# GpSimd walks the side chains' gathers three steps behind its slots, and TensorE waits for the selected rows sample by sample

## The chip, the cores and the metric

The kernel is one program on one core of a Trainium2 chip. The metric is device time in microseconds, the median of the runs; lower is better. The profiler's record of one execution gives the rows below.

## The reference

One layer of a decoder is computed for 512 prompt tokens and for 8 sample tokens, each sample with a paged cache of 4096 past tokens. Cut to what matters here:

```python
# samples: three attentions, each after a choice that depends on scores
score = einsum(relu(q_idx . k_idx_all) * w_idx);  top_i = top_k(score, 256)
kv = gather_paged(cache_a_kv, page_table, kv_a, top_i)         # branch A: 256 rows per sample
o_cmp, sel, sel_ok = nsa_compressed(q_b, qpos, kv_c, ...)      # compressed blocks, top 16 blocks
o_slc = nsa_selected(q_b, qpos, sel, ..., gather_paged(cache_slc_kv, ...))   # 16 blocks of 64 tokens
o_win = nsa_window(...); o_m = memory_attend(q_m, cache_mem_kv)
# prompt: expert retrieval, 512 tokens x 8 heads x 16 experts
a = gelu(einsum('nhkd,nd->nhk', u_tab[e], xb));  out = einsum('nhk,nhkd->nd', g * a, v_tab[e])
```

## The kernel before

**The slot stream.** The prompt's experts are mixed in 512 slots: 4 tiles of 128 tokens, 128 experts per token. For slot `s` GpSimd issues one indirect DMA (L3256) that brings, for each of the 128 tokens, one row of 8 KB (the expert's row of `u_tab` and of `v_tab` side by side), so 1.05 MB per slot. It lands in one of `NBUF` = 7 buffers, which lie in space that other tiles left (`ex_pairs`, `heads_t`, `branch_rows_t`, `cmp_k_t`, `cmp_v`); the rows call the gathers by these names. VectorE multiplies and sums the u half with the token (L3288, "the dot"), ScalarE makes the coefficient one step later, and `LAG` = 3 steps later the v half is added: by VectorE (L3283) or, for some slots, by TensorE with a diagonal matrix (L3350). A buffer is free when slot `s - 7` is dotted and added. So GpSimd can issue the gather of slot `s` as soon as the add of slot `s - 7` is done, which VectorE or TensorE does at its step `s - 4`: GpSimd runs up to four steps ahead.

**The side chains.** The rest of the layer is spread between the slots. `Beside` holds a chain of stages, each with a first and a last step; a stage is a generator per engine, which yields the fraction of its steps at which its next piece is due. At step `s` each engine first calls `advance(..., s)`, which emits all pieces due by then, and then does its own work of slot `s`. A stage begins with a wait for all engines that took part in the stages before it (`ended`). There are two chains, `beside` and `aside`; each engine runs its instructions strictly in order. From slot 317 on the chain `beside` is the samples' attention, and this is where GpSimd has pieces of its own:

- `INDEX` (28 steps): loads of index keys, `is_ch` (L2221), four at the stage's start, then 12 more, each into a ring of 4; TensorE transposes each of them. Chunk `u` is due on GpSimd at `(u - 1) / 17` of the stage, on TensorE at `(u + 0.5) / 17`.
- `SELECT` (36 steps): three iotas (L2362) for the 256 keys to be chosen, and from the end of it 16 small gathers `sk_t` (L2182, one step each), which VectorE reads in `place_keys` (L2470), 14 steps on.
- `da_rows`: 32 gathers of the chosen keys, values and biases (`da_kv`, `da_bias`), spread over `DSA_ROWS` = 30 steps; then 16 gathers `sl_bias`.
- `sl_gather`: 16 gathers of 0.52 MB each (`sl_kv`, and the last four into `cmp_k_t` and `cmp_v`), two per step over 8 steps, for the attention over the selected blocks, `sl_at` (`SEL_AT` = 40 steps). At its end GpSimd waits until all 16 have landed, and the next stages wait for GpSimd.
- on `aside`: two loads of the window's keys and values, 2.1 MB each (L2623), from slot 348 on, and later the ring of memory keys and values (L2662), 0.5 MB each.

Of `attend_samples` the change uses an argument that other calls use already:

```python
def turn(u):
    b, j, m = units[u]
    for sem, value in (waits(b) if waits else ()):
        pe.wait_ge(sem, value)
```

Of the kernel before, what the change touches and what calls it, by code (L numbers as in the profile page):

```python
# [19 lines left out]
SEQ, DB, PAST, PAGE = 512, 8, 4096, 128  # L20
# [5 lines left out]
DH, HQ, KV, GRP = 64, 8, 2, 4  # L26
# [5 lines left out]
BLK, NBLK, NSEL = 64, PAST // 64, 16  # L32
# [47 lines left out]
RETRIEVE_HALF, RETRIEVE_NEXT, MERGE, TURN, LINEAR, NORM, RETRIEVE_LAST = 22, 40, 64, 4, 16, 9, 64  # L80
WEIGHTS, COMPRESS, INDEX, SELECT = 6, 72, 28, 36
WINDOW_FROM, WIN_AT, MEMORY, CMP_AT, DSA_AT, SEL_AT = 348, 16, 70, 14, 18, 40
DSA_ROWS = 30
ROW_MOVES = 200
NBUF, NDIAG = 7, 4
LAG, SETTLE, RELOAD = 3, 4, 60
# [141 lines left out]
class Kernel:  # L228
# [1876 lines left out]
    def sample_dsa(self, ctx, sl_rows, sl_bias, sl_bias_rows, qz, nsa):  # L2105
            nc, i, s = self.nc, self.i, self.s
# [3 lines left out]
            kv = self.sb("da_kv", [P, 2, DB, KV * 2 * DH], F32, ctx)  # L2110
# [10 lines left out]
            with tmp:  # L2121
                prob = self.sb("cm_prob", [DB * HQ, NCH_S + DB], F32, tmp)
                sk = ExitStack()
                with sk:
                    chosen = self.select_keys(sk)
                    self.attend_samples("cm_at", NCMP_S, HQ, qz, keys=lambda b: self.kc_t[:, b, :NCMP_S],
                                        values=lambda b, j: self.vc[:min(P, NCMP_S - P * j), b, j].rearrange("p g d -> p (g d)"), acc=nsa, turned=False,
                                        bias=self.bias_cmp, prob=prob, gate=self.gate_bh[:, 0:1], add=True, behind=[windowed], steps=CMP_AT, scoring=0.3)
                    self.place_keys(chosen, phys, past_ix, is_new)
                rows_at = self.beside.next_step  # L2130
                landed = self.gather("da_rows", [(kv[:, n // DB, n % DB, :], i["cache_a_kv"].rearrange("n p w -> (n p) w"), phys[:, n:n + 1]) for n in range(2 * DB)]
                            + [(bias[:, n // DB, n % DB, :], s["bias_pos"], past_ix[:, n:n + 1]) for n in range(2 * DB)], apart=True, steps=DSA_ROWS, behind=windowed)
                self.pick_blocks(prob, sl_rows, sl_bias_rows)
                self.beside.next_step = rows_at + DSA_ROWS
            sl_bias_in = self.gather("sl_bias_rows", [(sl_bias[:, BLK * n:BLK * n + BLK], s["bias_head"].rearrange("h (b t) -> (h b) t", t=BLK), sl_bias_rows[:, n:n + 1])
                                                      for n in range(NSEL)], apart=True, steps=18)

# [4 lines left out]
            with nc.psum_tensor("da_h_ps", [P, 512], F32) as h_ps, self.block() as block:  # L2142
# [18 lines left out]
                def _(pe):  # L2161
# [4 lines left out]
                                values=lambda b, j: kv[:, j, b, KV * DH:], acc=out_a,  # L2166
                                waits=lambda b: landed if b == 0 else (), bias_t=lambda j: bias_a[:, DB * j:DB * j + DB].rearrange("p b h -> p (b h)"), own=0, own_bias=0, own_mask=own_hit,
                                out0=0, steps=DSA_AT, scoring=0.4)
            return sl_bias_in

    def gather(self, tag, jobs, depth=4, apart=False, steps=None, behind=None):

        sems = [self.gather_sem(f"{tag}_in{n}") for n in range(min(depth, len(jobs)))]
        landed = [(sem, 16 * len(range(n, len(jobs), depth))) for n, sem in enumerate(sems)]
        with self.block(steps or len(jobs) * 3 // 7, apart) as block:
            @block.gpsimd
            def _(pool):
                if behind:
                    pool.wait_ge(*behind)
                for n, (dst, table, rows) in enumerate(jobs):  # L2180
                    yield n / len(jobs)
                    pool.indirect_dma_start(out=dst, out_offset=None, in_=table,  # L2182
                                            in_offset=bass.IndirectOffsetOnAxis(ap=rows, axis=0)).then_inc(sems[n % depth], 16)
                if not apart:
                    for sem, count in landed:
                        pool.wait_ge(sem, count)
        return landed
# [298 lines left out]
    def sample_slc(self, rows, bias, bias_in, qz, nsa):  # L2486
        i = self.i
        ctx = ExitStack()
        NG = DB * KV
        with ctx:  # L2490
            kv_new = self.sb("sl_kv", [P, NG - 2 * KV, OCT * 2 * DH], F32, ctx)
            old = [x.rearrange("p (g w) -> p g w", g=KV) for x in self.compressed_space()]
            rows_of = [kv_new[:, n:n + KV] for n in range(0, NG - 2 * KV, KV)] + old
            kv = [x.rearrange("p g (d c j) -> p c j (g d)", c=2, j=OCT) for x in rows_of]
            self.gather("sl_gather", [(rows_of[n // KV][:, n % KV], i["cache_slc_kv"].rearrange("n q w -> (n q) w"), rows[:, n:n + 1]) for n in range(NG)],
                        steps=8, behind=(self.aside.ended, self.aside.before))
            dropped = self.sem("sl_dropped")
            with self.block() as block:
                @block.vector
                def _(dve):  # L2500
                    for sem, count in bias_in:
                        dve.wait_ge(sem, count)

                    dve.memset(bias[:, BLK * (NSEL - 1):], NEG).then_inc(dropped, 1)
            self.attend_samples("sl_at", NSEL * BLK, HQ, qz, keys=lambda b, j: kv[b][:, 0, j], values=lambda b, j: kv[b][:, 1, j], acc=nsa,
                                bias=bias.rearrange("p (q i) -> p i q", i=OCT), own=1, own_bias=1, own_mask=self.own_mask, gate=self.gate_bh[:, 1:2],
                                add=True, out0=4, steps=SEL_AT, scoring=0.65)

# [706 lines left out]
    def mix_prompt(self, idx, gate, dots, coef, pair, x, y, diag, y_ps, chosen, beside, aside, merged):  # L3215
# [12 lines left out]
        def at(n):  # L3228

            return n // SLOTS, n % SLOTS  # L3230
# [7 lines left out]
        with nc.Block() as block:  # L3238
            @block.gpsimd
            def _(pool):  # L3240
                for s in range(end):
                    beside.advance("gpsimd", pool, s)
                    aside.advance("gpsimd", pool, s)
                    if s < NS:
                        t, m = at(s)
                        if m == 0 or s == SLOTS // 2:
                            pool.wait_ge(chosen, t + 1 + (1 if s else 0))
                        if s == ROW_MOVES:
                            pool.wait_ge(beside.ended, merged)
                        if s >= NBUF:  # L3250
                            pool.wait_ge(dot_done, s - NBUF + 1)
                            if by_dve[s - NBUF]:
                                pool.wait_ge(acc_done, dve_upto[s - NBUF])
                            else:
                                pool.wait_ge(mix_done, pe_upto[s - NBUF])
                        pool.indirect_dma_start(out=pair(s), out_offset=None, in_=i["uv_tab"],  # L3256
                                                in_offset=bass.IndirectOffsetOnAxis(ap=idx[:, t, m:m + 1], axis=0)).then_inc(pair_in[s % NBUF], 16)
                beside.advance("gpsimd", pool, 10 ** 9)
                aside.advance("gpsimd", pool, 10 ** 9)
# [313 lines left out]
```

## Time and profile before

| | us |
|---|---|
| runs | 2791.97 median (2789.25, 2791.97, 2803.37) |
| the profiled execution | 2781.56, its span 2779.9 |
| VectorE busy | 1761.6 |
| TensorE busy (matmul) | 1812.3 |
| GpSimd busy | 864.9 |
| ScalarE busy | 670.4 |
| gathers by GpSimd, share of the 16 DMA engines' span | 52.0% |

Busy times are of the whole span. The slots run from 805 to 2632 us; ahead of them lie the prompt's projections and attention, behind them the samples' own experts. What is read below are therefore stretches: which engine or queue is full there, and what ends the idle time of the others.

### The profile page before, as it was taken

The page shows a single profiled execution, that of the slowest core. Times are in us where ns is not written, and L with a number is a line of the kernel's source. Part 1 is how long each engine was busy: PE and PEld are TensorE (multiplying, and loading weights), DVE is VectorE, ACT ScalarE, POOL GpSimd, SP SyncE. Part 2 cuts the span into 40 slices and gives each one's busy share as a digit, 9 for nine tenths or more (in the row PEclk, how much of TensorE's full clock was granted, in tenths as well). Part 3 has the DMA queues.
Part 4 walks back from the last instruction along what each step waited for, and adds up shares of the span by engine and source line. Part 5 has one row for each costly group of instructions (what it writes and reads, how often), then busy time and mean ns, then how long its engine had stood idle before and what let it go on. Part 6 is the DMA issues. An engine that isn't in the chain of part 4 may idle for free. (4 is left out here: it accounts for less than half of the span.)

```text
span 2779.9 us, 25050 instructions
## 1 busy us (share of the span) xinstructions
PE 1812.3 (65%) x6605; PEld 1000.1 (36%) x6605; DVE 1761.6 (63%) x3916; ACT 670.4 (24%) x2035; POOL 864.9 (31%) x829
## 2 busy tenths in 40 slices
PE   7999799699836738844467515665877533418374
PEld 3466476444412213312222114444743213304311
DVE  3343465711168967685789965666779688859813
ACT  2011266410113323321233211222222111214100
POOL 1000042200024723342353432221531477654301
PEclk9999799899969969977799957878568755555586
DMA  4122320043248989997998898996986799899863
GB/s 150 25 88 76 96 92 2 1 166 130 104 167 349 421 348 358 355 392 306 377 379 326 356 367 311 350 355 246 404 343 247 295 351 374 324 363 398 330 227 122
DMA packets 200920, 727.69 MB, mean 262 GB/s; under 512 B 39785, under 2 KB 83330, under 8 KB 133898
## 3 DMA queue, kind: packets, MB, share of 16 engines
q0 software_dynamic: 84384, 577.16, 52.0%
q1 hardware_dynamic: 115226, 144.70, 15.3%
q10 hardware_dynamic: 1168, 4.23, 0.4%
q8 instruction: 54, 0.88, 0.1%
q14 instruction: 88, 0.72, 0.1%
HBM read 717.42 MB, written 12.66 MB: 263 GB/s over the span
## 5 line engine op out<-in xcount | busy, mean ns | idle before, releaser
L3256 POOL DMA_INDIRECT ex_pairs<-in_uv_tab,e_idx x147 | 196.0, 1333 | 552.9 <-POOLq L3153 246.7
L3316 ACT ACTIVATE ex_coef<-ex_dots 128x1 f32<-128x1 f32 x512 | 103.6, 202 | 1046.8 <-DVE ex_dots L3288 953.9
L3256 POOL DMA_INDIRECT branch_rows_t<-in_uv_tab,e_idx x163 | 192.2, 1179 | 256.8 <-DVE heads_t L3283 160.4
L3256 POOL DMA_INDIRECT heads_t<-in_uv_tab,e_idx x146 | 186.0, 1274 | 268.4 <-DVE heads_t L3283 146.8
L1337 PE MATMUL cs_pp<-cs_ch,xn_t 128*128 128x256 f32 x512 | 146.3, 456 | 175.9 <-DMA cs_ch<-in_cache_cmp_kv 175.9
L3288 DVE CUSTOM_DVE_ANT_0 branch_rows_t<-branch_rows_t,heads_t 128x1024 f32<-128x1024 f32 x163 | 198.6, 1220 | 55.2 <-DMA branch_rows_t<-in_uv_tab,e_idx 50.3
L3288 DVE CUSTOM_DVE_ANT_0 ex_pairs<-ex_pairs,heads_t 128x1024 f32<-128x1024 f32 x147 | 179.5, 1222 | 60.9 <-DMA ex_pairs<-in_uv_tab,e_idx 58.9
L820 PE MATMUL in_acc<-in_w,xn_t 128*128 128x512 f32 (+7 forms) x560 | 208.1, 527 | 5.8 <-POOLq L178 4.0
L3288 DVE CUSTOM_DVE_ANT_0 heads_t<-heads_t 128x1024 f32<-128x1024 f32 x146 | 178.1, 1221 | 37.8 <-DMA heads_t<-in_uv_tab,e_idx 34.9
L1337 PEld LDWEIGHTS cs_pp<-cs_ch,xn_t 128*128 128x128 f32 x512 | 118.5, 235 | 205.9 <-DMA cs_ch<-in_cache_cmp_kv 106.8
L3283 DVE SCALAR_TENSOR_TENSOR heads_t<-branch_rows_t,ex_coef,heads_t 128x1024 f32<-128x1024 f32 x118 | 151.2, 1281 | 30.6 <-issue 14.7
L3318 ACT ACTIVATE ex_coef<-ex_coef,e_gate 128x1 f32<-128x1 f32 x512 | 150.8, 295 | 16.6
L3350 PE MATMUL ex_y_ps<-ex_pairs,heads_t 128*128 128x512 f32 x188 | 98.9, 657 | 76.9 <-ACT heads_t L3323 71.8
L3283 DVE SCALAR_TENSOR_TENSOR heads_t<-ex_pairs,ex_coef,heads_t 128x1024 f32<-128x1024 f32 x100 | 127.9, 1279 | 28.5 <-issue 24.9
L3283 DVE SCALAR_TENSOR_TENSOR heads_t<-heads_t,ex_coef 128x1024 f32<-128x1024 f32 x100 | 128.0, 1280 | 25.5 <-issue 22.2
L820 PEld LDWEIGHTS in_acc<-in_w,xn_t 128*128 128x128 f32 (+1 forms) x560 | 95.1, 174 | 108.3 <-issue 88.4
L3350 PE MATMUL ex_y_ps<-heads_t 128*128 128x512 f32 x184 | 99.0, 667 | 47.8 <-ACT heads_t L3323 38.6
L3350 PE MATMUL ex_y_ps<-branch_rows_t,heads_t 128*128 128x512 f32 x180 | 96.2, 666 | 31.8 <-ACT heads_t L3323 30.9
L1638 PE MATMUL at_t_ps<-at_diag,at_exp 128*128 128x128 f32 (+3 forms) x608 | 87.6, 288 | 21.7 <-POOL at_diag L1726 20.9
L2925 PE MATMUL fq_mg_g_ps<-fq_mg_wg,xn_t 128*128 128x512 f32 x192 | 85.0, 596 | 0.0
L3350 PEld LDWEIGHTS ex_y_ps<-ex_pairs,heads_t 128*128 128x128 f32 x188 | 35.6, 205 | 135.5 <-ACT heads_t L3323 97.8
L1638 PEld LDWEIGHTS at_t_ps<-at_diag,at_exp 128*128 128x128 f32 (+3 forms) x608 | 71.9, 185 | 34.6 <-POOL at_diag L1726 22.0
(727 smaller groups left out, 3435.1 us busy)
## 6 DMA issues: line engine op xcount, KB each, us to landing
cs_ch<-in_cache_cmp_kv SPq DMA_DIRECT2D x256, 128.0 KB
fq_mg_wg<-in_w_gate SPq DMA_DIRECT2D x6, 2048.0 KB
in_w<-in_w_in SPq DMA_DIRECT2D x4, 2048.0 KB, 11.3
first_w<-in_w_gate SPq DMA_DIRECT2D x3, 2048.0 KB, 7.9
fp_wb<-in_w_branch SPq DMA_DIRECT2D x6, 1024.0 KB, 10.2
fp_wg<-in_w_gate SPq DMA_DIRECT2D x3, 2048.0 KB, 8.1
fq_mg_wb<-in_w_branch SPq DMA_DIRECT2D x6, 1024.0 KB
fs_mg_wb<-in_w_branch SPq DMA_DIRECT2D x6, 1024.0 KB, 9.8
```

What stands on the lines that cost most here:

```text
L820: last = pe.matmul(acc[:r, u % 2, :n], self.xT[:, k, P * t:P * t + r], w[:, j % 2, k, :n], start=(k == 0), stop=(k == KD - 1))
L1337: last = pe.matmul(pp[:, n % 2, 256 * c:256 * c + 256].rearrange("p (g k m) -> p g k m", g=KV, m=8), wts[:, c, r, :], ch[:, n % NBUF, :, c ...
L1638: last = pe.matmul(t_ps[:w, u % 2, k, :], ex[:, u % 6, P * k:P * k + w], diag[:, u % 4, :], start=True, stop=True)
L2925: last = pe.matmul(g_ps[:r, u % 2, :], xT[:, k, cols], wg[j % depth][:, k, :], start=(k == 0), stop=(k == KD - 1))
L3256: pool.indirect_dma_start(out=pair(s), out_offset=None, in_=i["uv_tab"], in_offset=bass.IndirectOffsetOnAxis(ap=idx[:, t, m:m + 1], axis=0 ...
L3283: dve.scalar_tensor_tensor(out=y(t), in0=v(n), scalar=coef[:, t, m:m + 1], in1=y(t), op0=ALU.mult, op1=ALU.add).then_inc(acc_done, 1)
L3288: dve.tensor_tensor_reduce(out=u(s), in0=u(s), in1=x(t), scale=1.0, scalar=0.0, op0=ALU.mult, op1=ALU.add, accum_out=dots[:, t, m:m + 1]). ...
L3316: act.activation(c, dots[:, t, m:m + 1], ACT.Gelu_apprx_tanh).then_inc(gelu_done, 1)
L3318: act.activation(c, c, ACT.Copy, scale=gate[:, t, m:m + 1]).then_inc(coef_done, 1)
L3350: last = pe.matmul(y_ps[:, q, :], diag[:, (pe_upto[n] - 1) % NDIAG], v(n)[:, 512 * q:512 * q + 512], start=n in first_pe, stop=n in last_pe)
```

## The change

Three edits, all in the order of work.

GpSimd's pieces of both chains are emitted with `s - BEHIND` in place of `s`, so three slot gathers later than before. `beside` gets `LANDING` = 5 more steps between the start of `da_rows` and what follows it. `sl_gather` no longer holds GpSimd until its rows have landed: it is a stage apart, each sample has a semaphore of its own, TensorE waits for it before the sample's transposes, and what follows it is put `SEL_ROWS` = 12 steps on (8 before).

```diff
-DSA_ROWS = 30
+DSA_ROWS, SEL_ROWS, LANDING, BEHIND = 30, 12, 5, 3
@@ sample_dsa
-                self.beside.next_step = rows_at + DSA_ROWS
+                self.beside.next_step = rows_at + DSA_ROWS + LANDING
@@ gather
-    def gather(self, tag, jobs, depth=4, apart=False, steps=None, behind=None):
+    def gather(self, tag, jobs, depth=4, apart=False, steps=None, behind=None, sems=None):
-        sems = [self.gather_sem(f"{tag}_in{n}") for n in range(min(depth, len(jobs)))]
+        sems = sems or [self.gather_sem(f"{tag}_in{n}") for n in range(min(depth, len(jobs)))]
-                                            in_offset=bass.IndirectOffsetOnAxis(ap=rows, axis=0)).then_inc(sems[n % depth], 16)
+                                            in_offset=bass.IndirectOffsetOnAxis(ap=rows, axis=0)).then_inc(sems[n * len(sems) // len(jobs) if len(sems) == DB else n % depth], 16)
@@ sample_slc
+            kv_in = [self.gather_sem(f"sl_rows_in{b}") for b in range(DB)]
-                        steps=8, behind=(self.aside.ended, self.aside.before))
+                        depth=DB, sems=kv_in, apart=True, steps=8, behind=(self.aside.ended, self.aside.before))
+            self.beside.next_step += SEL_ROWS
-            self.attend_samples("sl_at", NSEL * BLK, HQ, qz, keys=lambda b, j: kv[b][:, 0, j], values=lambda b, j: kv[b][:, 1, j], acc=nsa,
+            self.attend_samples("sl_at", NSEL * BLK, HQ, qz, keys=lambda b, j: kv[b][:, 0, j], values=lambda b, j: kv[b][:, 1, j], acc=nsa, waits=lambda b: [(kv_in[b], 16 * KV)],
@@ mix_prompt, gpsimd
-                    beside.advance("gpsimd", pool, s)
-                    aside.advance("gpsimd", pool, s)
+                    beside.advance("gpsimd", pool, s - BEHIND)
+                    aside.advance("gpsimd", pool, s - BEHIND)
```

The first place where GpSimd's own order changes is the start of `INDEX`. Its rows there before (slot gathers at L3256, a row with x2 is two of them):

```order
L3256 DMA ex_pairs<-in_uv_tab,e_idx 128x2048 x2
L2221 DMA is_ch<-in_cache_a_kidx,chunk_rows 128x1024 x4
L3256 DMA heads_t<-in_uv_tab,e_idx 128x2048 x2
L3256 DMA branch_rows_t<-in_uv_tab,e_idx 128x2048 x3
L2221 DMA is_ch<-in_cache_a_kidx,chunk_rows 128x1024
```

And now, where the slot gathers have line L3258:

```order
L3258 DMA ex_pairs<-in_uv_tab,e_idx 128x2048 x2
L3258 DMA heads_t<-in_uv_tab,e_idx 128x2048 x2
L3258 DMA branch_rows_t<-in_uv_tab,e_idx 128x2048
L2221 DMA is_ch<-in_cache_a_kidx,chunk_rows 128x1024 x4
L3258 DMA branch_rows_t<-in_uv_tab,e_idx 128x2048 x2
L3258 DMA ex_pairs<-in_uv_tab,e_idx 128x2048 x2
L3258 DMA heads_t<-in_uv_tab,e_idx 128x2048
L2221 DMA is_ch<-in_cache_a_kidx,chunk_rows 128x1024
```

Three slot gathers (317 to 319) moved ahead of the first index loads, and with them ahead of the wait for the stage before; every later index load stands three gathers further down too. TensorE's and VectorE's orders are unchanged here.

The second place is the end of the 16 small gathers `sk_t` and the start of `da_rows`. Before, with the memory ring's loads (`xn_t`) between:

```order
L2182 DMA sk_t<-tmp_cand,sk_cand_at 128x1
L3256 DMA branch_rows_t<-in_uv_tab,e_idx 128x2048
L2662 DMA xn_t<-in_cache_mem_kv 128x1024
L3256 DMA branch_rows_t<-in_uv_tab,e_idx 128x2048
L2182 DMA da_kv<-in_cache_a_kv,da_phys 128x256
L3256 DMA ex_pairs<-in_uv_tab,e_idx 128x2048
```

Now:

```order
L2182 DMA sk_t<-tmp_cand,sk_cand_at 128x1
L3258 DMA ex_pairs<-in_uv_tab,e_idx 128x2048
L2664 DMA xn_t<-in_cache_mem_kv 128x1024
L3258 DMA heads_t<-in_uv_tab,e_idx 128x2048
L2182 DMA da_kv<-in_cache_a_kv,da_phys 128x256
L3258 DMA heads_t<-in_uv_tab,e_idx 128x2048
```

The last `sk_t` stood ahead of the gather of slot 397 and stands ahead of that of slot 400 now, while VectorE's `place_keys`, which reads it, keeps its place at step 396.

The third place is the start of `sl_gather`. Before:

```order
L3256 DMA branch_rows_t<-in_uv_tab,e_idx 128x2048 x2
L2182 DMA sl_kv<-in_cache_slc_kv,sl_rows 128x1024
L3256 DMA ex_pairs<-in_uv_tab,e_idx 128x2048
L2182 DMA sl_kv<-in_cache_slc_kv,sl_rows 128x1024 x2
L3256 DMA ex_pairs<-in_uv_tab,e_idx 128x2048
```

Now:

```order
L3258 DMA branch_rows_t<-in_uv_tab,e_idx 128x2048
L3258 DMA ex_pairs<-in_uv_tab,e_idx 128x2048
L2182 DMA sl_kv<-in_cache_slc_kv,sl_rows 128x1024
L3258 DMA ex_pairs<-in_uv_tab,e_idx 128x2048
L2182 DMA sl_kv<-in_cache_slc_kv,sl_rows 128x1024 x2
```

The first `sl_kv` stood ahead of the gather of slot 448 and stands ahead of that of slot 456 now: five steps by `LANDING`, three by `BEHIND`. The attention that reads the rows starts at step 466 in place of 457, and ends at step 506 in place of 497; the slots end at 511.

## Rows read from the trace of the kernel before

**Rows 1.** Windows: slots before and in the samples' attention, and one full stretch.
```profile
core 0: us, PE busy (x) PEld busy (x) DVE busy (x) ACT busy (x) POOL busy (x), PEclk, DMA share, GB/s
805.00:1912.00 1107.00, 655.69 (x1734) 315.15 (x1735) 828.25 (x1704) 299.16 (x873) 417.14 (x317) 0.81 0.92 358
1912.00:2632.00 720.00, 389.74 (x1399) 260.25 (x1397) 559.75 (x1041) 163.16 (x562) 350.78 (x312) 0.60 0.86 337
1956.00:2035.00 79.00, 72.07 (x336) 69.88 (x336) 71.86 (x113) 18.67 (x62) 40.80 (x34) 0.50 1.02 419
```

**Rows 2.** Waits of GpSimd: line, what for, us in total, times, longest.
```profile
POOL is_ch L2221 <- DVEq L177: 31.7, 1, 31.7
...
POOL xn_t L2662 <- DVEq L177: 19.0, 1, 19.0
...
POOL sk_grid_i L2362 <- POOLq L178: 15.5, 1, 15.5
...
POOL sl_kv L2182 <- DVEq L177: 11.7, 1, 11.7
...
POOL sk_t L2182 <- DVEq L177: 7.3, 1, 7.3
```

**Rows 3.** Windows around these stalls, and one behind the third, columns as in Rows 1.
```profile
1920.00:1950.00 30.00, 14.93 (x60) 11.00 (x60) 16.03 (x40) 7.39 (x15) 5.14 (x6) 0.74 0.23 60
2042.00:2055.00 13.00, 8.29 (x16) 4.16 (x16) 8.80 (x38) 2.70 (x9) 2.44 (x5) 0.63 0.19 35
...
2140.00:2157.00 17.00, 7.56 (x35) 4.93 (x34) 15.44 (x48) 3.71 (x13) 0.51 (x1) 0.78 0.13 48
...
2167.00:2195.00 28.00, 14.48 (x25) 5.49 (x26) 19.62 (x55) 6.79 (x23) 4.99 (x5) 0.70 0.81 327
...
2420.00:2440.00 20.00, 0.40 (x4) 0.29 (x4) 10.34 (x19) 1.99 (x8) 6.45 (x8) 0.50 0.57 211
```

**Rows 4.** Timeline of VectorE, dots that waited: start, us, what, idle before.
```profile
1956.47 1.23 DVE L3288 CUSTOM_DVE_ANT_0 heads_t<-heads_t 128x1024 f32<-128x1024 f32 x1 [5.28 <-DMA heads_t<-in_uv_tab,e_idx]
...
2074.28 1.23 DVE L3288 CUSTOM_DVE_ANT_0 branch_rows_t<-branch_rows_t,heads_t 128x1024 f32<-128x1024 f32 x1 [9.73 <-DMA branch_rows_t<-in_uv_tab,e_idx]
...
2167.14 1.23 DVE L3288 CUSTOM_DVE_ANT_0 branch_rows_t<-branch_rows_t,heads_t 128x1024 f32<-128x1024 f32 x1 [9.47 <-DMA branch_rows_t<-in_uv_tab,e_idx]
...
2213.89 1.23 DVE L3288 CUSTOM_DVE_ANT_0 branch_rows_t<-branch_rows_t,heads_t 128x1024 f32<-128x1024 f32 x1 [4.28 <-DMA branch_rows_t<-in_uv_tab,e_idx]
...
2221.77 1.22 DVE L3288 CUSTOM_DVE_ANT_0 branch_rows_t<-branch_rows_t,heads_t 128x1024 f32<-128x1024 f32 x1 [2.58 <-DMA branch_rows_t<-in_uv_tab,e_idx]
...
2440.50 1.23 DVE L3288 CUSTOM_DVE_ANT_0 ex_pairs<-ex_pairs,heads_t 128x1024 f32<-128x1024 f32 x1 [7.16 <-DMA ex_pairs<-in_uv_tab,e_idx]
...
2484.49 1.22 DVE L3288 CUSTOM_DVE_ANT_0 ex_pairs<-ex_pairs,heads_t 128x1024 f32<-128x1024 f32 x1 [5.32 <-DMA ex_pairs<-in_uv_tab,e_idx]
```

**Rows 5.** Timeline of GpSimd: last `sk_t`; gathers of slots 398 and 456.
```profile
2254.56 0.95 POOL L2182 DMA_INDIRECT sk_t<-tmp_cand,sk_cand_at  x1 [0.30 <-issue]
...
2258.03 0.97 POOL L3256 DMA_INDIRECT branch_rows_t<-in_uv_tab,e_idx  x1 [0.30 <-issue]
...
2478.22 1.77 POOL L3256 DMA_INDIRECT ex_pairs<-in_uv_tab,e_idx  x1 [15.30 <-DVE ex_dots L3288]
```

**Rows 6.** Timeline of VectorE: `place_keys` reads `sk_t`.
```profile
2261.85 0.18 DVE L2470 TENSOR_SCALAR da_is_new<-sk_t 128x16 f32<-128x16 f32 x1 [1.47 <-DMA sk_t<-tmp_cand,sk_cand_at]
```

**Rows 7.** Timeline of GpSimd and VectorE: the gather of slot 338, and its dot.
```profile
2012.52 1.36 POOL L3256 DMA_INDIRECT heads_t<-in_uv_tab,e_idx  x1 [1.84 <-DVE heads_t L3283]
...
2024.81 1.22 DVE L3288 CUSTOM_DVE_ANT_0 heads_t<-heads_t 128x1024 f32<-128x1024 f32 x1
```

**Rows 8.** Timeline: an add, the last scores of `sl_at`, and the VectorE instruction behind.
```profile
2552.98 1.28 DVE L3283 SCALAR_TENSOR_TENSOR heads_t<-branch_rows_t,ex_coef,heads_t 128x1024 f32<-128x1024 f32 x1
...
2554.13 1.12 PE L1954 MATMUL sl_at_l_ps<-sl_at_kt,sample_qz 128*64 128x128 f32 x4
...
2555.46 2.03 DVE L2037 TENSOR_TENSOR sl_at_p<-sl_at_l_ps,sl_bias 64x512 f32<-64x512 f32 x2
```

## The prediction

> **What bounds the kernel now.** I read windows first, because the busy shares of the whole span mix stages. From 805 to 1912 us, before the samples' attention, the 16 DMA engines are 0.92 busy and VectorE 828 of 1107 us: transfers set the pace, GpSimd has no pieces of its own there, and the change moves nothing. From 1912 to 2632 the same two are at 0.86 and 560 of 720 us [rows 1]. No engine is full, DMA is not either, so the stretch holds gaps in which both stand still; TensorE, 390 of 720, is further off. In the full part of it, 1956 to 2035, DMA is at 1.02 with 419 GB/s and VectorE at 71.9 of 79 us [rows 1]: that is what the stretch looks like when nothing stalls.
>
> The waits come next. GpSimd waits once for each stage that it enters: 31.7 us for `is_ch` (`INDEX`), 19.0 for `xn_t` (the memory ring), 15.5 for `sk_grid_i` (`SELECT`), 11.7 for `sl_kv`, 7.3 for `sk_t` [rows 2]. Behind each stands the next slot gather. Windows around four such places show the DMA share at 0.23, 0.19, 0.13 and 0.57, the memory ring's being the emptiest [rows 3]; GpSimd's wait alone costs nothing, an empty DMA queue does. What it costs is read on VectorE, as the idle time that a dot spends on its rows: 5.28 us at 1956, 9.73 at 2074, 9.47 at 2167, 4.28 and 2.58 at 2214 and 2222, 7.16 at 2440, 5.32 at 2484 [rows 4]. The last of these follows GpSimd's hold for the 16 landings: its gather of slot 456 was issued after 15.30 us of idle time [rows 5].
>
> **The change, part by part.** With `BEHIND` = 3 GpSimd issues three more slot gathers before it comes to the same wait. The wait still ends when VectorE or TensorE end their stage, so GpSimd waits less, and DMA has 3 x 1.05 MB more to move meanwhile: at 419 GB/s that is 7.5 us of transfers. Where DMA is the pace behind the stall, 7.5 us bounds the gain; where it isn't, what bounds it is three slots' pace. From the dot of slot 317 (1956.47) to that of 338 (2024.81) a slot takes 68.3 / 21 = 3.25 us [rows 4, 7], so three are 9.8.
>
> The Trainium skill, page "DMA: Bandwidth & Descriptors", section "Where 436 GB/s comes from", puts the limit for transfers between HBM and SBUF at the HBM side, about 358 GB/s per core. By it three gathers would be 8.8 us, and the second term below 8.8 in place of 7.5, a sum 1.3 larger. The trace disagrees, with 419 GB/s over 79 us [rows 1], so I stay with 7.5.
>
> - `INDEX`: VectorE's idle time is 5.28 [rows 4], less than 7.5. Gain 5.3. Bounds: 2 (if the rest of the queue refills more slowly) and 7.5.
> - `SELECT`: idle 9.73, in front of it the window's two loads of 2.1 MB, which still stand ahead of slot 351's gather in the queue. So not the whole idle time goes: gain 7.5, the three gathers. Bounds 4 and 9.7.
> - Memory ring: idle 9.47 [rows 4], and behind it DMA is at 0.81 only [rows 3], so not the bound. Three slots' pace (9.8) covers it. Gain 9.5. Bounds 5 and 9.8.
> - First `sk_t`: 4.28 + 2.58 = 6.9 [rows 4], within 7.5. Bounds 3 and 7.5.
> - `sl_gather`: GpSimd comes to it later by three slots and by `LANDING`'s five steps, when what it waits for is over, and no longer holds for the landings. 7.16 + 5.32 = 12.5 [rows 4]. `LANDING` itself is free as long as slots are left to cover the attention that starts nine steps later: it ends at step 506 of 511. Bounds 7 (if TensorE and VectorE, which work in 9 steps fewer after it, give the landing part back) and 13.
>
> Sum of gains 41.7.
>
> Costs. The last `sk_t` was issued at 2254.56 and read by `place_keys` at 2261.85, after 1.47 us of waiting: 7.3 us from issue to use [rows 5, 6]. Now it stands behind the gather of slot 399, whose buffer is free after the add of step 395; the gather of 398 went out at 2258.03 [rows 5], and a step of dot and add is 1.23 + 1.28 = 2.5 us [rows 4, 8]: 2260.5, and with the same 7.3 us it is read at 2267.8, 6 late. VectorE stands still for it, with the dot behind. Meanwhile gathers go on, which gives back 1 by my estimate: cost 5. Bounds: 0 (the buffers fill, and VectorE catches up) and 9 (DMA's queue is longer by three gathers and the small one waits 1.5 + 7.5).
>
> TensorE now waits per sample in `sl_at`, in front of 64 groups of transposes. Scoring is a chain on TensorE at the granted clock 0.5, that is 1.2 GHz; its last matmul begins at 2554.13 and is followed at 2555.46 by the VectorE instruction that reads it [rows 8], so nothing is spare there. A wait that is long over costs TensorE a fraction of 0.1 us in a sequence with 64 of them: cost 1, between 0 and 4. The landed rows themselves have nine further steps, so the wait itself stays empty. In return GpSimd's hold goes, which is in the last gain.
>
> The other edits, which semaphore each `sl_kv` counts on, cost nothing: they are a number in an instruction that is there anyway.
>
> Sum: 41.7 - 5 - 1 = 35.7 us off the profiled execution of 2781.56: 2745.9. Its time stands 0.37% below the median of the runs shown, 2791.97; times that ratio, 2756.
>
> **The rivals.** *Waits go to VectorE.* The pieces that GpSimd issues late are read on time by others. If late landings at `INDEX` and at `sk_t` take back half of the first four gains (29.2 / 2 = 14.6), the gain is 21.1, the time 2771. For it: `place_keys` waits already now [rows 6]. Against it: the stages are 14 steps from issue to use elsewhere.
>
> *DMA is full anyway.* If the gathers that are issued ahead only stand longer in a queue that moves no more bytes, 2792. Against it: shares of 0.13 to 0.57 at the very places [rows 3]. For it: the share is 0.86 over the whole stretch [rows 1], and behind every stall the backlog is worked off at full rate.
>
> *More gain.* The buffers stay fuller behind each place, and small waits for gathers go too, of which 720 - 560 = 160 us of VectorE's idle time [rows 1] has many that I didn't count. If they give another 20, 2736.
>
> *The index ring starves (slower).* Chunk `u` is due on TensorE 1.5 / 17 of 28 steps, 2.5 steps, after GpSimd; with the four steps that GpSimd runs ahead this is 6.5, and three of them go. 3.5 slots x 3.25 = 11.4 us are left. A gather takes 12.3 us from issue to its dot, 2012.52 to 2024.81 [rows 7]: if a chunk takes as long in the queue, it is 0.9 late. From there VectorE (which copies each transpose) stops, its buffers aren't freed, and GpSimd issues the next chunk later still. With 12 refills it decides from (35.7 + 14) / 12 = 4.1 us each. At 5 us each the time is 2781.56 - 35.7 + 60, scaled 2816. Against it: the 12.3 hold time in which the rows had landed and the dot only waited its turn.
>
> The Trainium skill says on the same page, section "Two DMAs through the same engine are not ordered", that descriptors of one queue start in order, which would give a chunk the whole wait of the gathers ahead of it and speaks for this rival. The trace has a small `sk_t` landed 7.3 us after issue at the latest [rows 5, 6], with the gather of slot 397 and others around it, which is neither proof nor disproof.
>
> **How the numbers follow.** The forecast case has 60%, waits on VectorE 16%, DMA full anyway 8%, more gain 8%, the index ring 8%. 0.5% is 14 us and about what a measurement of this kernel tells from no change. The forecast's own range is 2742 to 2770: gains at their lower bounds together would be 21, but not all at once, and above by 13. Over all cases 2735 to 2782 leaves out the ring, the full queue and part of the "more gain" case. Faster by over 0.5% (below 2778): the 60, the 8 of more gain, and 13 of the 16. Within 0.5%: 3 and the 8 of the full queue. Slower: 8.
>
> **What the profile would show.** Right, if: GpSimd's waits for `is_ch`, `sk_grid_i` and `xn_t` shrink by about 10 us each and the DMA shares of [rows 3] rise; the idle time before the dots of [rows 4] goes, with 2 to 3 us left at the window's loads; `place_keys` waits 6 to 8 us in place of 1.47; GpSimd has no idle time of 15 us at its last `sl_kv`; the stretch of 720 us is about 36 shorter, and the one before it unchanged. Wrong, if: TensorE's transposes of `is_ch` wait for their DMA, 12 times, with VectorE's copies behind; or the idle time on VectorE is the same in sum and only named otherwise; or the slots end earlier but `sl_at`, nine steps later, still runs behind them, so that the end doesn't move.

## The result, and the profile after

The changed kernel takes 2774.52 us (median of 20 runs, 2755.52 to 2791.53) against 2789.56 (20 runs); the ratio is 0.9945, interval 0.9926 to 0.9964. Timed again later it was 0.9934 (0.9907 to 0.9960). It is faster, by 15 to 18 us where 35.7 were forecast.

GpSimd's waits, the view of [rows 2], in the profile after:

```profile
POOL is_ch L2221 <- DVEq L177: 18.3, 1, 18.3
...
POOL xn_t L2664 <- DVEq L177: 10.9, 1, 10.9
...
POOL sk_grid_i L2362 <- POOLq L178: 9.1, 1, 9.1
...
POOL sk_t L2182 <- DVEq L177: 0.6, 1, 0.6
```

They shrank as forecast: by 13.4, 8.1 and 6.4 us. The wait for `sl_kv` is gone, and of that for `sk_t` 0.6 us is left. Windows, columns as in [rows 1]; the last is the loading of the selected rows:

```profile
805.00:1912.00 1107.00, 641.19 (x1717) 305.90 (x1719) 817.53 (x1688) 296.00 (x865) 411.14 (x311) 0.81 0.90 354
1912.00:2632.00 720.00, 385.25 (x1417) 261.00 (x1413) 576.70 (x1064) 166.97 (x571) 361.89 (x317) 0.60 0.88 343
...
2144.00:2157.00 13.00, 9.66 (x47) 6.20 (x45) 10.73 (x30) 3.45 (x12) 3.44 (x4) 1.00 0.99 384
2240.00:2258.00 18.00, 4.22 (x20) 1.98 (x18) 6.20 (x9) 1.50 (x6) 11.46 (x11) 0.76 1.00 393
2440.00:2490.00 50.00, 0.00 (x0) 0.00 (x0) 29.46 (x39) 5.97 (x24) 29.69 (x30) 0.50 1.02 411
```

DMA, at 0.13 ahead of the memory ring in [rows 3], is at 0.99 in nearly the same microseconds. Two new readings stand beside it. The stretch to 1912 us, where the two kernels run the same instructions, was slower here (354 GB/s, 311 gathers in place of 317). And VectorE waits at places where it did not before, or longer than before; its timeline, as in [rows 4]:

```profile
1959.76 1.28 DVE L3285 SCALAR_TENSOR_TENSOR heads_t<-branch_rows_t,ex_coef,heads_t 128x1024 f32<-128x1024 f32 x1 [4.76 <-DMA is_w<-tmp_w]
1960.96 1.22 DVE L3290 CUSTOM_DVE_ANT_0 heads_t<-heads_t 128x1024 f32<-128x1024 f32 x1
...
2062.53 0.48 DVE L1881 MEMSET sample_qz<- 128x512 f32 x1 [6.42 <-SPq L177]
...
2089.86 1.23 DVE L3290 CUSTOM_DVE_ANT_0 ex_pairs<-ex_pairs,heads_t 128x1024 f32<-128x1024 f32 x1 [5.54 <-DMA ex_pairs<-in_uv_tab,e_idx]
...
2163.94 1.22 DVE L3290 CUSTOM_DVE_ANT_0 branch_rows_t<-branch_rows_t,heads_t 128x1024 f32<-128x1024 f32 x1
...
2260.48 0.17 DVE L2470 TENSOR_SCALAR da_is_new<-sk_t 128x16 f32<-128x16 f32 x1 [10.44 <-DMA sk_t<-tmp_cand,sk_cand_at]
...
2428.76 1.23 DVE L3290 CUSTOM_DVE_ANT_0 ex_pairs<-ex_pairs,heads_t 128x1024 f32<-128x1024 f32 x1 [0.58 <-DMA ex_pairs<-in_uv_tab,e_idx]
...
2467.72 1.23 DVE L3290 CUSTOM_DVE_ANT_0 branch_rows_t<-branch_rows_t,heads_t 128x1024 f32<-128x1024 f32 x1 [2.59 <-DMA branch_rows_t<-in_uv_tab,e_idx]
```

The dots of slots 317 (1960.96) and 370 (2163.94) no longer wait for their rows, and that of 448 (2428.76) waits 0.58, where [rows 4] has 5.28, 9.47 and 7.16. `place_keys` waits 10.44 where [rows 6] has 1.47. The wait of 4.76 in the first line is not new. In the kernel before it was longer:

```profile
1949.90 1.29 DVE L3283 SCALAR_TENSOR_TENSOR heads_t<-branch_rows_t,ex_coef,heads_t 128x1024 f32<-128x1024 f32 x1 [6.13 <-DMA is_w<-tmp_w]
```

**Where the time went.** The cleanest measure is the start of each dot in the two traces, slot by slot. From the dot of slot 316, ahead of the first moved instruction, to that of 511 it is 698.0 us before and 675.0 after, 23.1 shorter by the unrounded times. By place, forecast beside it (negative is faster):

| slots | place | forecast | measured |
|---|---|---|---|
| 316 to 317 | start of `INDEX` | -5.3 | -6.7 |
| 317 to 344 | inside `INDEX` | 0 | +5.6 |
| 344 to 345 | hand-over to `SELECT` | 0 | +3.4 |
| 345 to 351 | start of `SELECT`, window loads | -7.5 | -9.0 |
| 351 to 369 | rest of `SELECT` | 0 | 0.0 |
| 369 to 381 | memory ring | -9.5 | -5.7 |
| 381 to 394 | `sk_t` | -6.9 | -9.0 |
| 394 to 396 | `place_keys` | +5 | +8.7 |
| 396 to 447 | `da_rows`, `da_at` | 0 | -3.1 |
| 447 to 466 | `sl_gather` | -12.5 | -10.8 |
| 466 to 511 | `sl_at` and rest | +1 | +3.4 |
| sum | | -35.7 | -23.1 |

Inside `INDEX` it is TensorE that waits for late chunks, and at the hand-over VectorE, for SP's queue. Waits (us in total, times, longest), before and after:

```profile
PE is_tr L2234 <- DMA is_ch<-in_cache_a_kidx,chunk_rows: 6.9, 2, 5.2
...
DVE sample_qz L1881 <- SPq L177: 3.3, 1, 3.3
```

```profile
PE is_tr L2234 <- DMA is_ch<-in_cache_a_kidx,chunk_rows: 19.1, 10, 5.2
...
DVE sample_qz L1881 <- SPq L177: 6.4, 1, 6.4
```

At the hand-over `SELECT` waits until the scores' store `tmp_score` has landed. Instructions on that tile, and from its DMA to landing, before and then after:

```profile
L2211 SPq DMA_DIRECT2D tmp_score<-is_score x1: 385/385/385, 2045.9 to 2045.9; - x1
...
DMA to landing us min/median/max: 3.0/3.0/3.0
```

```profile
L2211 SPq DMA_DIRECT2D tmp_score<-is_score x1: 385/385/385, 2056.2 to 2056.2; - x1
...
DMA to landing us min/median/max: 6.1/6.1/6.1
```

Before, the store went out while GpSimd stood still. Now it shares the DMA engines with slot gathers. Windows from its issue to its landing, before and then after:

```profile
2045.90:2048.90 3.00, 1.50 (x2) 0.10 (x1) 0.00 (x0) 0.45 (x2) 0.00 (x0) 0.80 0.42 44
```

```profile
2056.20:2062.30 6.10, 3.45 (x4) 0.84 (x3) 0.00 (x0) 0.23 (x1) 0.04 (x1) 0.50 0.83 235
```

44 GB/s over 3.0 us are 0.13 MB, the store itself; 235 GB/s over 6.1 us are 1.43 MB, so that 1.3 MB of other transfers passed with it.

### The profile page after: what moved, and what is told of

Its sections match the earlier page's. It is cut to its first block and busy times, and to the rows that moved or that the text cites. A ratio compares the mean times of both kernels' runs of the same rounds, so it can differ in the third digit from the quotient of the medians.

```text
span 2769.0 us, 25110 instructions
## 1 busy us (share of the span) xinstructions
PE 1790.5 (65%) x6605; PEld 988.9 (36%) x6605; DVE 1760.9 (64%) x3916; ACT 671.4 (24%) x2035; POOL 871.7 (31%) x829
## 3 DMA queue, kind: packets, MB, share of 16 engines
q1 hardware_dynamic: 115226, 144.70, 15.3%
## 5 line engine op out<-in xcount | busy, mean ns | idle before, releaser
L3258 POOL DMA_INDIRECT ex_pairs<-in_uv_tab,e_idx x147 | 190.8, 1298 | 560.8 <-POOLq L3155 244.4
L3258 POOL DMA_INDIRECT heads_t<-in_uv_tab,e_idx x146 | 186.8, 1279 | 303.2 <-DVE heads_t L3285 196.9
L3258 POOL DMA_INDIRECT branch_rows_t<-in_uv_tab,e_idx x163 | 195.8, 1201 | 251.7 <-DVE heads_t L3285 176.0
L1337 PE MATMUL cs_pp<-cs_ch,xn_t 128*128 128x256 f32 x512 | 136.9, 434 | 193.8 <-DMA cs_ch<-in_cache_cmp_kv 193.8
L1337 PEld LDWEIGHTS cs_pp<-cs_ch,xn_t 128*128 128x128 f32 x512 | 112.1, 222 | 221.1 <-DMA cs_ch<-in_cache_cmp_kv 123.3
L3285 DVE SCALAR_TENSOR_TENSOR heads_t<-heads_t,ex_coef 128x1024 f32<-128x1024 f32 x100 | 128.0, 1280 | 26.2 <-issue 21.9
```

Of the source, the lines that this page charges most:

```text
L1337: last = pe.matmul(pp[:, n % 2, 256 * c:256 * c + 256].rearrange("p (g k m) -> p g k m", g=KV, m=8), wts[:, c, r, :], ch[:, n % NBUF, :, c ...
L3285: dve.scalar_tensor_tensor(out=y(t), in0=v(n), scalar=coef[:, t, m:m + 1], in1=y(t), op0=ALU.mult, op1=ALU.add).then_inc(acc_done, 1)
```

## Experiments

Theory A below: the stalls' gaps are won, and the late pieces of `INDEX` and `sk_t` cost more than I charged. Theory B, the rival: the gain is the `sl_gather` edit alone. For each run the ratio to before with its interval and the stretch from dot 316 to dot 511 (before: 698.0; after: 675.0) are given.

**`BEHIND` = 0.**

```diff
-DSA_ROWS, SEL_ROWS, LANDING, BEHIND = 30, 12, 5, 3
+DSA_ROWS, SEL_ROWS, LANDING, BEHIND = 30, 12, 5, 0
```

> The changed kernel with BEHIND = 0: GpSimd's pieces stand where they stood before, and LANDING, SEL_ROWS and the waits per sample stay. Theory A (BEHIND removes the gaps at INDEX, SELECT, memory ring and sk_t, about 31 us, and gives 18 back because the index refills and the last sk_t come late; the sl_gather edit is worth about 13): here the four gaps are back (VectorE idle 5, 10, 9 and 7 us before those dots), place_keys waits 1.5 us again, the stretch from the dot of slot 316 to that of 511 is about 13 shorter than before, ratio to before about 0.9955. Theory B (the whole gain is the sl_gather edit, BEHIND nets nothing): the same ratio as the changed kernel, 0.9945, within 0.002. The two are near each other in time; the profile's idle times decide.

Ratio 0.9993 (0.9976 to 1.0010), stretch 696.1. Both theories missed. Between the slots 420 and 447 it gains 3.5 us, and between 447 and 456 another 12.5, GpSimd's hold being gone. Between 456 and 466 it loses 9.0, because the selected rows' transfers only moved, and by 495 another 3.2, as the changed kernel does too (3.8). Theory B falls, and so does the 13 that A gave this edit by itself.

**`BEHIND` alone.**

```diff
-DSA_ROWS = 30
+DSA_ROWS, SEL_ROWS, LANDING, BEHIND = 30, 12, 0, 3
...
                 for s in range(end):
-                    beside.advance("gpsimd", pool, s)
-                    aside.advance("gpsimd", pool, s)
+                    beside.advance("gpsimd", pool, s - BEHIND)
+                    aside.advance("gpsimd", pool, s - BEHIND)
```

> The kernel before with BEHIND = 3 alone: LANDING = 0, sl_gather holds GpSimd until the rows have landed, as before. Theory A: gaps at INDEX, SELECT, ring and sk_t gone (31 us) and 18 back; the start of sl_gather comes three gathers later (7 gained of the 12.5 there), its landing still holds GpSimd. Stretch from slot 316 to 511 about 20 shorter, ratio about 0.993. Theory B: 0 to 3 us, ratio 0.999 to 1.001.

Ratio 1.0021 (1.0003 to 1.0039), stretch 693.7. Theory A missed by 0.9%. Theory B, with at most 1.001, was nearer, but neither had the two losses that this run shows. The gaps are won as in the changed kernel (14.5 us between the slots 345 and 350, 7.4 at 370), but 8.8 are lost between 420 and 447, at a place that I had priced at nothing. The wait of VectorE there, in this run:

```profile
DVE da_bias_a L2152 <- DMA da_bias<-tmp_bias_pos,da_past_ix: 6.7, 1, 6.7
```

`da_rows` comes three gathers late, and what reads it stood with no slack. The changed kernel has no such wait: `LANDING` covers it.

A second loss in this run is larger. VectorE begins its next stage (L2504) at step 456, and that stage waits for the end of GpSimd's `sl_gather`. VectorE's timeline there, in the kernel before and then in this run:

```profile
2477.47 0.11 DVE L2504 MEMSET sl_bias<- 64x64 f32 x1 [0.21 <-POOLq L178]
```

```profile
2495.28 0.11 DVE L2504 MEMSET sl_bias<- 64x64 f32 x1 [15.31 <-POOLq L178]
```

With GpSimd three gathers later, its hold for the 16 landings stops VectorE for 15.3 us, where before it was over in time. Between 447 and 466 only 0.6 us are gained.

**`LANDING` = 0 in the changed kernel.**

```diff
-DSA_ROWS, SEL_ROWS, LANDING, BEHIND = 30, 12, 5, 3
+DSA_ROWS, SEL_ROWS, LANDING, BEHIND = 30, 12, 0, 3
```

> The changed kernel with LANDING = 0. Theory A: da_bias lands late for VectorE (as where BEHIND stood alone: 6.74 us of idle time before L2152), 8 to 9 us are lost between the slots 420 and 447, and the stretch from dot 316 to dot 511 is 683 to 686 us in place of 675; the start of sl_gather, three gathers behind its slots, still gains. Rival: LANDING only moves sl_gather; then 675 again, within 2.

Ratio 0.9971 (0.9950 to 0.9992), stretch 692.3. The wait is there, 6.8 us, in this run too; 10.5 us are lost between 420 and 447, and 13.5 in place of 10.8 won between 447 and 466. The stretch is 17.4 us longer than the changed kernel's, but 9.4 of them stand ahead of slot 420, where both kernels run the same instructions in the same order, so that they can't come from the edit. Behind slot 420 it is 8.0 us, and by the ratios 7 to 10: that is what `LANDING` is worth with `BEHIND`, the 8 to 9 of the expectation.

This run and the one before it differ in the `sl_gather` edit alone (`SEL_ROWS` with it). From slot 447 to 466 it makes 12.9 us (13.5 won against 0.6), and by the ratios 0.5% (0.9971 against 1.0021, from separate comparisons). So the parts don't add: `BEHIND` alone +0.2%, the rest alone -0.1%, together -0.6%. The two edits need each other.

```profile
DVE da_bias_a L2152 <- DMA da_bias<-tmp_bias_pos,da_past_ix: 6.8, 1, 6.8
```

**Index refills at their old steps, then the `sk_t` gathers too.** The stages' starts stay three gathers behind.

```diff
                         if u >= NBUF:
-                            yield (u - 1) / (NU + 1)
+                            yield (u - 1) / (NU + 1) - BEHIND / INDEX
...
-                    yield n / len(jobs)
+                    yield n / len(jobs) - early
...
-            picked = self.gather("sk_pick", ..., apart=True, steps=16)
+            picked = self.gather("sk_pick", ..., apart=True, steps=16, early=BEHIND / 16)
```

> The changed kernel, with the 12 index refills emitted at their old steps (their fraction is less by 3 of 28 steps), the first four still three gathers later. Theory A: TensorE's waits for is_ch fall from 19 us to about 7, the idle time on VectorE behind them (some 9 us between the dots of slots 317 and 345) goes, 9 us faster than the changed kernel, ratio to before about 0.991. If instead the transfers are the bound there (DMA share 0.98 to 1.02), the refills only change places with the slot gathers: VectorE then waits for its gathers in place of TensorE for is_ch, and the ratio stays 0.9945.

> As the run with the index refills at their old steps, and the sk_t gathers too (fraction less by 3 of 16 steps): only the stages' starts are behind. Theory A: place_keys waits 1.5 to 3 us for sk_t in place of 10.4, 8 us more, 17 faster than the changed kernel, ratio to before about 0.988 to 0.989. If the wait before place_keys was only a place where VectorE's lead was given back (the gathers are the bound), it moves to the dots behind 396 and the ratio is that of the run with the index refills alone.

> The kernel with the index refills and the sk_t gathers at their old steps once more, timed on one chip beside the changed kernel. Theory A: stretch 316 to 511 668 us, ratio to before 0.990 to 0.991, 6 to 8 us below the changed kernel. Rival: the difference lies in one profile only, both at 0.9935.

The first (refills alone): ratio 0.9933 (0.9901 to 0.9964), stretch 675.0. TensorE's wait for chunks is down to what it was before, VectorE's at the hand-over is longer:

```profile
PE is_tr L2234 <- DMA is_ch<-in_cache_a_kidx,chunk_rows: 6.3, 2, 6.1
...
DVE sample_qz L1881 <- SPq L177: 8.3, 1, 8.3
```

Between dots 317 and 344 it gains 0.9 on before, where the changed kernel loses 5.6: late refills are shown as the cause of that loss. But 5.0 us are lost at slot 345 in place of 3.4, the gain from there to slot 420 is 3.2 smaller and that behind it 1.2, so that the stretch is that of the changed kernel. That these later losses follow from the edit is not shown: in six profiles with the same order of instructions up to slot 420 (the changed kernel three times, and the runs with `BEHIND` alone, with `LANDING` at 0 and with the waits at once) the stretch up to there is 4 to 14 us shorter than before. The store in this run:

```profile
L2211 SPq DMA_DIRECT2D tmp_score<-is_score x1: 385/385/385, 2047.6 to 2047.6; - x1
...
DMA to landing us min/median/max: 8.0/8.0/8.0
```

Both: ratio 0.9919 (0.9898 to 0.9940), timed again 0.9881 (0.9861 to 0.9901); stretch 668.3 and 669.3. VectorE's wait for `sk_t` is gone, the slots 394 to 396 are 1.3 us faster than before in place of 8.7 slower, and nothing of that moves to the dots behind; 3 of the 10 come off the gain at 381 to 387. This version beats both kernels: 2761.4 us both times, the second time 29.5 us below before and some 13 below the changed kernel timed beside it (2774.14). Of the 17 us that I expected on top of the changed kernel the first stretch shows 7. That they are won, and not scatter, is seen from both: up to slot 420 they are 20.6 and 19.9 us shorter than before, more than any of the six profiles above.

**`INDEX` as before, and four gathers in place of three.** The first emits pieces at `s` up to step 345 and at `s - 3` from 346 on, the second has `BEHIND = 4`; both with refills and `sk_t` at their old steps.

```diff
+                    back = BEHIND if s >= 346 else 0
-                    beside.advance("gpsimd", pool, s - BEHIND)
+                    beside.advance("gpsimd", pool, s - back)
```

> Only the start of each stage is three gathers behind, and only from step 346 on: INDEX as before, the sk_t gathers at their old steps. Theory A, amended: behind the first stall the transfers are the bound (DMA share 1.02 in the stretch behind), so that the 5 to 7 us gained at dot 317 are given back by dot 345; then INDEX as before costs nothing, the stretch 316 to 511 is 29 to 31 us shorter than before, ratio 0.989 to 0.992, as with both at their old steps. Rival: the give-back is the price of late refills alone; then the kernel with INDEX's start ahead is better, and this one is 5 to 6 slower than it, ratio 0.994.

> The kernel with index refills and sk_t at their old steps, and four gathers ahead at the stages' starts in place of three (four is as far as the 7 buffers let GpSimd run). Theory A: each gather ahead fills a gap with 2.5 us of transfers where DMA runs dry: another 2 to 4 us at SELECT and at the memory ring, nothing elsewhere; da_at and sl_at, whose rows come a step later, take 0 to 3 back. Ratio 0.001 below that of three, 0.991 to 0.990. Rival: GpSimd meets its buffers' ends and the pieces go late: 5 us slower than with three.

`INDEX` as before: ratio 0.9895 (0.9867 to 0.9923), stretch 679.1. The two disagree: by the ratio nothing is lost, by the trace 11 us (2.0 lost at slot 317, where those that start `INDEX` behind three gathers gain 4 to 7, and 4.8 at 345). What the start of `INDEX` is worth stays open. The trace does show the hand-over again: `tmp_score` lands after 7.7 us and VectorE waits 8.0, though in this kernel `INDEX` is untouched. The three gathers that pass ahead of `SELECT`'s start suffice. Over all profiles the store lands after 3.0 us where GpSimd keeps its old steps (three profiles), after 6.1 to 9.0 with three gathers ahead (ten), and after 10.7 with four.

Four gathers: ratio 0.9902 (0.9875 to 0.9929), stretch 671.5, no gain over three. The wait at slot 351 is gone, but 5.7 us are lost by slot 369, and VectorE waits 11.0 at the hand-over.

**TensorE's waits all ahead of the first sample.**

```diff
-waits=lambda b: [(kv_in[b], 16 * KV)]
+waits=lambda b: [(sem, 16 * KV) for sem in kv_in] if b == 0 else ()
```

> The changed kernel with all four of TensorE's waits for the selected rows ahead of the first sample's transposes, none per sample. What I charged for the wait per sample was 1 us; if the rows have all landed by step 466, as theory A has it, the stretch 316 to 511 stays 675, within 1, and the 3 to 4 us lost between the slots 466 and 495 stay. Rival: the semaphore waits stretch TensorE's chain; then 3 us less there.

Ratio 0.9928 (0.9902 to 0.9953), stretch 673.7, and 3.1 us lost between 466 and 495 as in the changed kernel (3.8). When TensorE waits makes no difference. The run does not show what the waits cost. There are eight semaphores, not four, one for each sample, and in this edit TensorE waits for all eight at each of the first sample's eight groups: 64 waits, as many as in the changed kernel. What settles it is the length of the scoring chain, with and without waits. Instructions on its two tiles, with first and last start, before (no waits) and then after (64 waits):

```profile
L1949 PE MATMUL sl_at_kt_ps<-ident,sl_kv x48: 418/477/478, 2489.6 to 2537.3; 128*128 128x128 f32 x48
...
L1954 PE MATMUL sl_at_l_ps<-sl_at_kt,sample_qz x128: 421/421/476, 2490.5 to 2554.8; 128*64 128x128 f32 x128
```

```profile
L1949 PE MATMUL sl_at_kt_ps<-ident,sl_kv x48: 421/477/479, 2498.5 to 2546.1; 128*128 128x128 f32 x48
...
L1954 PE MATMUL sl_at_l_ps<-sl_at_kt,sample_qz x128: 417/421/476, 2499.3 to 2563.7; 128*64 128x128 f32 x128
```

From the first transposes to the last scores it is 65.2 us in both.

**Both kernels once more**, for the scatter.

> The kernel before once more, for a second profile. Up to the dot of slot 316 the two kernels run the same instructions, and yet the changed kernel's dot 316 came 11.2 us later (1946.0 against 1934.8), with TensorE and DMA of the compressed keys (cs_ch) in between. If this is scatter from one execution to the next, the dot of slot 316 lies here at another place between 1930 and 1950, while the stretch from it to the dot of 511 is 698 us again, within 3. If it is a cost of the change, it is 1935 again here.

> The changed kernel once more. If the lateness ahead of slot 316 is scatter, the dot of slot 316 lies anywhere between 1930 and 1957; if the change causes it, it is at 1945 or later again. The stretch from dot 316 to dot 511 is 675 us as in its first profile (23 less than before), within 3, on either account.

> The changed kernel once more, timed beside the one above. Its stretch was 23.0 and 21.9 us shorter than the first profile of before; its ratio 0.9945 (15 us). If the 8 us between the two are scatter, ratio here 0.991 to 0.994 and the dot of slot 316 below 1946 as often as above; if they are a loss ahead of slot 316, 0.9945 again with dot 316 at 1946.

| | before, twice | changed, three times |
|---|---|---|
| dot of slot 316 | 1934.8, 1942.0 | 1946.0, 1946.9, 1945.1 |
| stretch 316 to 511 | 698.0, 701.0 | 675.0, 676.2, 682.1 |

The stretch is 21.7 us shorter in the mean, and 15 to 18 us are left by the ratio. What is between them stands ahead of slot 316. In all 14 profiles of this study each engine's instructions up to there are in the same order, and dot 316 lies between 1934.8 and 1956.7. TensorE's waits for the compressed keys' loads vary. Its timeline before, and then after, at the one ahead of the dot of slot 276:

```profile
1747.48 10.15 PE L1337 MATMUL cs_pp<-cs_ch,xn_t 128*128 128x256 f32 x32 [5.79 <-DMA cs_ch<-in_cache_cmp_kv]
```

```profile
1761.09 8.91 PE L1337 MATMUL cs_pp<-cs_ch,xn_t 128*128 128x256 f32 x32 [20.80 <-DMA cs_ch<-in_cache_cmp_kv]
```

Scatter of this size is shown by kernels that share `BEHIND` = 3 (1936.9 to 1956.7). But the four in which GpSimd keeps its old steps up to there (before twice, `BEHIND` = 0, and `INDEX` as before) have 1938.4 in the mean, the ten others 1945.4, and no mechanism for a difference was found. The last run does not decide it: its ratio is as expected for scatter, its dot 316 at 1945.1 as expected for a loss. Whether 7 us of it belong to the change is open.

## Why the prediction was off

**Right in its mechanism.** DMA ran dry at each stage that GpSimd waited for, and gathers issued ahead filled that: GpSimd's waits, the DMA shares and the dots behind `INDEX`, `SELECT`, ring and `sk_t` moved as described. The four gains were forecast at 29.2 and measured at 30.4 (6.7 + 9.0 + 5.7 + 9.0). At `SELECT` 5.5 us stayed at the window's loads (2 to 3 forecast). That the sizes came out near is in part luck: the sum left out waits of the same kind. Two stand ahead of the 9.73 at `SELECT`, on the dots of slots 346 and 347, and one at `sk_t`, on that of slot 393. VectorE's timeline before:

```profile
2058.77 1.22 DVE L3288 CUSTOM_DVE_ANT_0 heads_t<-heads_t 128x1024 f32<-128x1024 f32 x1 [2.60 <-DMA heads_t<-in_uv_tab,e_idx]
...
2061.92 1.22 DVE L3288 CUSTOM_DVE_ANT_0 branch_rows_t<-branch_rows_t,heads_t 128x1024 f32<-128x1024 f32 x1 [1.92 <-DMA branch_rows_t<-in_uv_tab,e_idx]
...
2252.22 1.22 DVE L3288 CUSTOM_DVE_ANT_0 ex_pairs<-ex_pairs,heads_t 128x1024 f32<-128x1024 f32 x1 [5.27 <-DMA ex_pairs<-in_uv_tab,e_idx]
```

With them `SELECT` had 14.3 us to win, of which 14.5 went by slot 350 and 5.5 came back, and the first `sk_t` came out at 9.0, above its upper bound of 7.5. The memory ring gave 5.7 of 9.5.

**The step that failed first** is "DMA has 3 x 1.05 MB more to move meanwhile", read as free for everybody but the slots. What was emitted behind those gathers, and what shared the queues with them, came late, and three times it was read by something without slack:

- Inside `INDEX`: +5.6, forecast 0 in the sum. I had it as a rival: "3.5 slots x 3.25 = 11.4 us are left" against 12.3 needed, priced at 8% because only its ruinous form changes the sign. The mechanism was real at a tenth of that price. It belonged in the sum. Rival 1, whose half of 14.6 us goes back on VectorE, gave 2771, and was nearest.
- At the hand-over to `SELECT`: +3.4. I didn't look at the small store on SP's queue, since it is on no line of the diff. It lands in 3.0 us before and in 6.1 to 9.0 with three gathers ahead.
- `place_keys`: charged 5, measured 8.7. The 7.3 us from issue to use held (6.9: 2253.54 to 2260.48). Off was when the issue comes. GpSimd needs about 1.25 us for each, and in the changed kernel it issues one after the other there; its timeline:

```profile
2249.17 1.57 POOL L3258 DMA_INDIRECT branch_rows_t<-in_uv_tab,e_idx  x1 [0.30 <-issue]
2251.04 0.95 POOL L2182 DMA_INDIRECT sk_t<-tmp_cand,sk_cand_at  x1 [0.30 <-issue]
2252.30 0.94 POOL L3258 DMA_INDIRECT ex_pairs<-in_uv_tab,e_idx  x1 [0.30 <-issue]
2253.54 0.95 POOL L2182 DMA_INDIRECT sk_t<-tmp_cand,sk_cand_at  x1 [0.31 <-issue]
```

VectorE came to `place_keys` at 2260.48 - 10.44 = 2250.04, when the last but one was not yet out; the last was issued 3.5 us later. I had it issued at the moment when VectorE comes. In the kernel before, VectorE was itself held up by its dots there.

Together these three are 12.7 us (5.6 + 3.4 + 3.7 beyond the 5 charged), as much as lies between 35.7 and the 23.1 of the trace; the table's other differences cancel. What the ratio shows less than the trace, 5 to 8 us, stands ahead of slot 316 and stays open.

**`sl_gather`.** The sum's 12.5 was near (10.8), but its reason was incomplete. "no longer holds for the landings" is worth next to nothing by itself: the run without `BEHIND` gave back within ten slots most of what it had gained. In the window of the changed kernel DMA is at 1.02 there, and each dot waits 2.6 us, as it did in the kernel before over as many slots. The gathers ahead are worth nothing here by themselves either: with the hold still there VectorE stood 15.3 us. Only both together gain, and `LANDING` does not make this gain but keeps 10.5 us from being lost ahead of it. "`LANDING` itself is free" was right in its price and blind to its use.

**TensorE's waits**: no row showed the 1 us that was charged, a fraction of 0.1 us for each of 64. The scoring chain takes 65.2 us with and without them, so their cost is about nothing.

**The DMA limit.** The Trainium skill, page "DMA: Bandwidth & Descriptors", section "Where 436 GB/s comes from", puts the limit for transfers between HBM and SBUF at about 358 GB/s per core. The changed kernel moves 411 over 50 us, so the trace again stands against it.

## What to carry to other kernels

Work issued ahead of a stall fills the stall, and delays everything that is emitted or queued behind it. So list every transfer in the next stages, with its slack from issue to reader, and let only the stage's first wait be passed: pieces that have a reader soon keep their step. Price a near miss (0.9 us short, twelve times) into the sum instead of leaving it to a rival that needs a catastrophe. A hold can be worth nothing by itself and still be in the way of another edit: look at which stage waits for its end. And before a difference between two profiles is put down to an edit, see how much of it stands where both run the same instructions.

## What was unexpected

A store of 128 KB took 3.0 us to land beside an idle GpSimd, 6.1 to 9.0 where three gathers of 1.05 MB had been issued ahead from another engine's queue, and 10.7 with four. Identical instructions up to slot 316 took from 1934.8 to 1956.7 us, a spread of 21.9 us, larger than the gain of 15 to 18.
